# Decoder step on one core: the first cache pages asked for one weight block later, and two heads' rows read ahead of the fourth decay

## The reference

```python
u = x * (1.0 + sc1) + sh1                       # adaLN modulate
z = u @ lw['w_in'] + lw['b_in']                 # one combined input projection
# four mixers: A mLSTM (4 heads), B latent attention (8 heads), C causal conv of width 31, D retention (4 heads)
# B for a sample sequence reads 8 pages of 128 cached rows: past = cache_mla[l][page_table]
proj = jnp.einsum('btnw,nwd->btnd', ys, lw['w_branch'])
g = jax.nn.sigmoid(gates.reshape(B, T, N_BRANCH, D_MODEL))
out = jnp.sum(g * proj, axis=2) @ lw['w_out']
x = layer_norm(DEEPNORM_ALPHA * x + g1 * mix, ...)
f = (jax.nn.silu(u2 @ lw['w1']) * (u2 @ lw['w3'])) @ lw['w2']
x = layer_norm(DEEPNORM_ALPHA * x + g2 * f, ...)
```

## Time and profile before

| | us |
|---|---|
| median of three runs (lowest 1889.52, highest 6953.5) | 1890.94 |
| the profiled execution, device time | 1886.14 |
| its span from first to last instruction | 1884.1 |
| TensorE matmul busy | 1710.7 |
| VectorE / ScalarE / GpSimd busy | 802.6 / 735.0 / 700.6 |
| granted TensorE clock, mean, share of full | 0.958 |

### The profile page before, as it was taken

The page is one execution under the profiler, slowest core; times in us unless marked ns, Lnnn a source line. Parts: engine busy times, 40 slices in busy tenths (PEclk is TensorE's granted clock), DMA queues, the critical chain, the costliest instruction groups (busy, mean ns, idle before and its releaser), DMA issues.

```text
span 1884.1 us, 30317 instructions
## 1 busy us (share of the span) xinstructions
PE 1710.7 (91%) x10994; PEld 1474.3 (78%) x10994; DVE 802.6 (43%) x1887; ACT 735.0 (39%) x1110; POOL 700.6 (37%) x438
## 2 busy tenths in 40 slices
PE   3899999998799989999839999999987999899997
PEld 1788899886378869999717888998854778699996
DVE  1454376654431353332324544865544313533223
ACT  1456534333434334443214564442234442444332
POOL 0444555554023433333113445555540234233331
PEclk9899999999899989999968999999999999899999
DMA  9242335256764344444072523362667653444440
GB/s 355 100 179 99 101 108 202 90 175 252 284 244 176 141 174 155 157 144 147 23 290 90 187 90 101 107 203 89 201 253 291 235 195 112 181 155 157 139 152 29
DMA packets 73246, 309.10 MB, mean 164 GB/s; under 512 B 15554, under 2 KB 25090, under 8 KB 43010
## 3 DMA queue, kind: packets, MB, share of 16 engines
q1 hardware_dynamic: 73090, 307.09, 45.4%
HBM read 291.81 MB, written 15.25 MB: 163 GB/s over the span
## 4 chain that ended last, share of the span: by engine, by line
PE 40%; DVE 4%; DMA 3%; issue 1%; ACT 1%; SPq 1%; DVEq 0%; ACTq 0%
PE zps L429 5%; PE zps L413 5%; PE zps L434 5%; PE zps L430 4%; PE zps L891 4%; PE zps L892 4%; PE zps L890 4%; DMA ring<-wpack_dram 2%; PE mps L413 1%; PE mps L736 1%; DVE arena L1689 1%; PE mps L760 1%; DMA arena<-cache_dram 1%; SPq L973 1%; PE zps L463 1%
## 5 line engine op out<-in xcount | busy, mean ns | idle before, releaser
L2015 POOL TENSOR_TENSOR wlx<-ring,wh 128x1024 fp32r<-128x1024 f32 x172 | 409.3, 2380 | 733.7 <-ACT wh L1046 728.8
L429 PE MATMUL zps<-uhi,wh 128*128 128x320 f32 x1232 | 382.9, 323 | 3.4 <-ACT wh L1046 1.7
L430 PE MATMUL zps<-ulo,wh 128*128 128x320 f32 x1232 | 370.1, 313 | 0.0
L1046 ACT ACTIVATE wh<-ring 128x1024 fp32r<-128x1024 f32 x172 | 182.3, 1060 | 386.8 <-PE zps L430 267.9
L2115 POOL TENSOR_TENSOR wlo<-ring,whi 128x1024 fp32r<-128x1024 f32 x66 | 160.2, 2427 | 311.0 <-ACT whi L1046 310.2
L429 PEld LDWEIGHTS zps<-uhi,wh 128*128 128x128 f32 x1232 | 236.9, 192 | 16.1 <-issue 9.3
L430 PEld LDWEIGHTS zps<-ulo,wh 128*128 128x128 f32 x1232 | 237.0, 192 | 0.8
L890 PE MATMUL zps<-xhi,whi 128*128 128x320 f32 x688 | 213.7, 311 | 0.0
L891 PE MATMUL zps<-xlo,whi 128*128 128x320 f32 x688 | 213.3, 310 | 0.0
L892 PE MATMUL zps<-xhi,wlo 128*128 128x320 f32 x688 | 213.2, 310 | 0.0
L434 PE MATMUL zps<-uhi,wlx 128*128 128x320 f32 x1248 | 210.5, 311 | 0.0
(11 more groups left out here) (279 smaller groups left out, 2541.5 us busy)
## 6 DMA issues: line engine op xcount, KB each, us to landing
ring<-wpack_dram SPq DMA_DIRECT2D x222, 1024.0 KB, 4.9
arena<-cache_dram SPq DMA_DIRECT2D x128, 320.0 KB, 4.8
arena<-stateA_dram SPq DMA_DIRECT2D x2, 2064.0 KB, 9.7
o_cn_s<-arena SPq DMA_DIRECT2D x2, 2064.0 KB, 11.1
arena<-stateD_dram SPq DMA_DIRECT2D x2, 2048.0 KB, 12.2
o_ret_s<-arena SPq DMA_DIRECT2D x2, 2048.0 KB, 11.6
x<-o_y SPq DMA_DIRECT2D x2, 1280.0 KB, 9.1
o_y<-x SPq DMA_DIRECT2D x4, 640.0 KB, 3.0
```

The lines of the kernel that those rows point to most:

```text
L429: nc.tensor.matmul(o, hi[:, k * P:(k + 1) * P], xh[:, k, :], start=k == 0, stop=False)
L430: last = nc.tensor.matmul(o, hi[:, k * P:(k + 1) * P], xl[:, k, :], start=False, stop=False)
L1046: return nc.scalar.activation(out, in_, func, **kw).then_inc(*ev(sem, label))
L2015: G().tensor_tensor(wlx[:, n % RING, half], ring[:, n % RING, half], wh[:, i, :], ALU.subtract).then_inc(*ev("pool_l", (q, i)))
```

## The change

Two lines move. On SP, the eight pages of sequence 0 are asked for behind the load of block SLOT_START[0] instead of ahead of it: the list changes from block (branch 3 4), pages 0, block (g2_0), block (ada 8), pages 1 to block (branch 3 4), block (g2_0), pages 0, block (ada 8), pages 1. On VectorE, the first head_rows changes places with the fourth decay. No instruction is added or removed on any engine, and no wait is changed.

```diff
-                        if BLOCKS[n] == ("branch", 3, 4):
+                        if n == SLOT_START[0]:
                             load_pages(0)
...
                     weigh("a", 2)
+                    head_rows("a", 0, W)
                     decay(3)
-                    head_rows("a", 0, W)
```

## The result

Median of the runs after 1869.2 us (1863.29 to 1869.31), of the kernel before on the same chip 1892.97. These two medians differ by 23.8 us, a ratio of 0.9874; the ratio on record, here and in the experiments, is not formed from the medians, and it is 0.9864 with a 95% interval of 0.9845 to 0.9884. The forecast was 1871.5 with a range of 1862 to 1883. The profiled execution took 1869.28 (span 1867.3) against a forecast of 1866.7 for it, and the mean granted clock is 0.960. TensorE is busy for 1706.9 us, 91% of the span.

The account below looks back on a forecast made before the run. TensorE was taken to bound the kernel. Gains of 4.3 and 5.4 us a layer, 19.4 in both, gave 1866.7 for the profiled execution; adding 4.8 to reach the median gave 1871.5, range 1862 to 1883.

Parts of the forecast that it names:

- TensorE bounds the kernel, and both waits cost time and clock: Whole span: TensorE busy 1710.7 of 1884.1 us; waits of 2.6 us (L582) and 4.8 us (L413), each with slower clock behind.
- Part A, 4.3 us a layer: Mixer, head_rows ahead of the fourth decay: the 2.6 us wait before head 3's scores goes, worth 4.3 us a layer.
- the lower bound of 2.5: Part A's gain per layer in us if the new 1.45 us wait for weigh 3 at the second outputs drops the clock.
- From here VectorE sets the pace: From the second outputs to TensorE's wait at 1229.83, VectorE's line, 4.27 us earlier, decides; TensorE still waits 1.1 us there.
- rival 4: VectorE's L1689 and GpSimd's subtractions meet differently: one meeting more or less is 2.2 us a layer, 1867.1 or 1875.9; chance 0.06.
- Part B, block in time: Dense block: block (g2_0) issued at 1357.27, 3.8 us earlier, lands at 1362.2, so the wait goes with 2.3 us to spare.
- Part B, 5.4 us a layer: Pages 0 behind block (g2_0): sample_scores(0) starts 5.4 us earlier in each layer; bounds 6.5 and 3.9.
- the new wait for pages 0: At sample_scores(0): pages of sequence 0 land at 1374.0, 1.1 us after TensorE is ready, with no clock loss added.
- Later pages: Pages 1 land at 1383.6, 1.8 us before sample_scores(1) wants them; later pages move with TensorE.
- Rival 5: Slower: the queue from pages 0 on is the bound and sample_scores(1) waits; 8.5 us a layer slower, 1908; chance 0.02.
- Sum: Whole kernel: 4.3 + 5.4 = 9.7 us a layer, 19.4 in both; profiled execution 1866.7.
- The 4.8 carried over from the profile before to the median: Whole kernel: the median is 4.8 us above the profiled execution; carried over, 1866.7 becomes the forecast 1871.5.

Follow-up runs that it names:

- experiment 6: The changed kernel with weigh 3 ahead of the rotate of dk1 instead of behind it: 1867.78 us, ratio 0.9864 to the kernel before.
- 7: The changed kernel with two unused reductions of 0.7 us each added on VectorE ahead of the head norm: 1871.23 us, ratio 0.9898 to the kernel before.
- experiment 5: The changed kernel with pages 0 asked for one block later still, behind block (ada 8): 1895.39 us against 1893.26 for the kernel before, ratio 1.0002.
- experiment 3: The kernel before, pages still ahead of the block, with sequence 0's eight page numbers read earlier, behind the branch state's write: 1884.75 us, ratio 0.9958.

## Why the prediction was right, point by point

- **TensorE bounds the kernel, and both waits cost time and clock:** right. Both waits went, each with its slow stretch.
- **Part A, 4.3 us a layer:** 4.2 and 4.1. TensorE's gain at the second outputs was put at 4.07 and the new wait there at 1.45; the wait was 1.25. The clock behind it stayed at 1.00 (window of 1176 to 1178), so the lower bound of 2.5 did not come.
- **"From here VectorE sets the pace":** this step failed, although its number was near. VectorE's own line, 4.27 us earlier, was to decide. In experiment 6 TensorE came 1.4 us earlier against VectorE's line, in 7 that line was given 1.41 us more, and TensorE's wait stayed at 1.28 to 1.29, since the held L1689 took it up. What decides is the end of GpSimd's subtraction, which keeps step with TensorE. So TensorE's gain upstream passes through the place as it is, in the prediction's terms 4.07 and not 4.27. The two differ by so little that the time could not show it; rival 4 had the right pair of engines, but took them for two lines that may meet or miss by 2.2 us.
- **Part B, block in time:** right in each term. Issue 0.17 us behind the tile's end, as said; landing in 5.2 us for 4.9; a dense block of 8.77 for 8.88.
- **Part B, 5.4 us a layer:** it was 6.5, the upper bound. The mis-sized term is the new wait for pages 0, put at 1.1 us and measured at 0.37 and 0.17. The first page went out 5.72 us behind the block instead of 6.20, and the scores started 9.96 us later instead of 10.5. Over seven kernels and both layers, this second time is 9.96 to 11.8 us wherever the scores waited, so 10.5 was a fair value, and the range of the wait, 0.2 to 2.0 us, is its spread. By the rule of the Trainium skill (DMA: Bandwidth & Descriptors, the sections on one DMA's anatomy and on bandwidth) the estimate was 9.3 us and Part B 6.5. The size of B came out near that, but not by that rule: the measured times of 9.96 to 11.8 all lie above 9.3, and every one of these scores waited.
- **Later pages:** right, sequence 1 has no new wait. Rival 5 had the right bottleneck at the wrong distance: experiment 5 shows the loss when pages 0 go one block later.
- **Sum:** 9.7 us a layer, 19.4 in all. Measured at the first scores it was 10.7 and 10.6. In the second layer 1.4 came on top ahead of them, by the clock, and 2.0 behind, where waits for later pages (0.91 and 1.51) are not in the trace after. But the first layer gave 2.1 back by its end, the second 4.6 at its conv norm, and 1.0 was lost at the start of the span, ahead of any change. So this pair of executions gained 16.9, and 1869.28 stands 2.6 above the 1866.7 that was forecast for it. The 2.0 and the 4.6 come with the profile before, as told above, and none of the others was traced to the change.
- **The 4.8 carried over from the profile before to the median:** this term failed. It is the distance of one execution from the median of three, and that execution was a fast one: 2.4 to 3.0 us of it lie in the slots, the rest has not been located. The profile after lies 0.1 from its median. So the forecast of 1871.5 took 2.2 us too little for Part B and added 4.8 that did not come; against the median measured with it, 1892.97, the gain was 23.8 and not 19.4. That 1871.5 lies so near 1869.2 is in part these errors against each other.

## What to carry to other kernels

Ask of a transfer when it is issued and what stands ahead of it in its queue, the reads of its addresses included: those can be done early, and here the page numbers, read while nothing was due, brought the first scores of each layer some 2 us forward in the traces, as much as one reordering of engine work; the times can't confirm so little. When a line of instructions ends last, look whether one of them is stretched by another engine; if it is, shortening the line only shortens the stretch, and the line to follow is that other engine's. Before you put a loss between two traces down to your change, look at the same place in the traces of the other kernels: here a stretch that ran 4.6 us slower after than before was slow in all traces but the one before. And ask how a profiled execution stands to the median of its kernel before you carry the difference over.

## What the runs showed of the hardware

- A VectorE instruction of 0.35 us (L1689) lasted 2.33, 0.82 and 0.90 us in three orders of the work, each time ending within 0.1 us of the end of GpSimd's 2.4 us subtraction, and so did all 78 that lay beside one. The Trainium skill (GPSIMD Engine Reference, Specifications) says that the two share SBUF interfaces; the traces agree and add what it cost here.
- A read of a page number on SyncE takes 0.27 us, in the first 9 us behind the issue of a 2 MB write to DRAM 0.9 at the median and up to 1.8.
- A block's issue takes 0.33 to 0.67 us around these places; 3.6 us behind the 2 MB write it took 4.00 and 3.98, and 3.70 and 3.81 in the first layers.
- The length of a wait alone does not tell whether the clock falls. After a wait of 1.25 to 1.3 us the clock stayed at 1.00 in some places and fell to 0.65 in others; after the waits of 2.6, 2.8 and 7.8 us that are told of above it fell; after the waits of 2.27 and 3.08 us of experiment 3 it stayed at 1.00.
